# Feed-forward's last group: where the running sum of squares is added

## The reference

```python
def rmsnorm(x, g):
    y = x * rsqrt(mean(x * x, axis=-1) + EPS)
    return y * g

def swiglu(x, w_gate, w_up, w_down):
    return (silu(x @ w_gate) * (x @ w_up)) @ w_down

# layer
x = x + 0.5 * swiglu(rmsnorm(x, n_f1), f1_g, f1_u, f1_d)
h = rmsnorm(x, n_mix)
...                       # two mixers of h, merged
x = x + merged @ w_o
x = x + 0.5 * swiglu(rmsnorm(x, n_f2), f2_g, f2_u, f2_d)
# end
y = rmsnorm(x, norm_final)
```

## Time and profile before

| what | value |
|---|---|
| median of 3 timed runs | 3586.05 us (3582.97 to 3590.58) |
| the profiled execution | 3583.59 us |
| its span, from the first to the last instruction | 3581.8 us |
| TensorE busy | 3382.4 us, 94% of the span |
| VectorE busy | 1156.0 us, 32% |
| ScalarE busy | 1000.0 us, 28% |
| GpSimd busy | 935.5 us, 26% |
| mean granted TensorE clock | 0.959 |

### The profile page before, as it was taken

The page is one execution under the profiler, slowest core; times in us unless marked ns, Lnnn a source line. Parts: engine busy times, 40 slices in busy tenths (PEclk is TensorE's granted clock), DMA queues, the critical chain, the costliest instruction groups (busy, mean ns, idle before and its releaser), DMA issues. The chain is left out here.

```text
span 3581.8 us, 52005 instructions
## 1 busy us (share of the span) xinstructions
PE 3382.4 (94%) x20610; PEld 3291.5 (92%) x20610; DVE 1156.0 (32%) x1780; ACT 1000.0 (28%) x1461; POOL 935.5 (26%) x520
## 2 busy tenths in 40 slices
PE   6999999996999799999999999769997999999997
PEld 6999999996999699999999999649997999999996
DVE  4232223224566333232232222142323232223223
ACT  5111111114333344444354342220123111111112
POOL 3112121214222323333233331211235112221212
PEclk8999999998999899999999999559998999999998
DMA  3111111102222212121121220245412111111101
GB/s 122 47 35 53 41 41 41 47 18 88 81 84 91 66 50 71 50 69 52 57 77 45 62 64 23 68 138 184 142 42 59 48 41 47 41 47 41 38 26 50
DMA packets 274431, 222.74 MB, mean 62 GB/s; under 512 B 12043, under 2 KB 251787, under 8 KB 274289
## 3 DMA queue, kind: packets, MB, share of 16 engines
q1 hardware_dynamic: 273988, 220.56, 20.4%
q10 hardware_dynamic: 324, 0.41, 0.0%
HBM read 170.66 MB, written 50.28 MB: 62 GB/s over the span
## 5 line engine op out<-in xcount | busy, mean ns | idle before, releaser
L163 PE MATMUL ffn_bank<-ffn_h_hi,ffn_w_hi 128*128 128x368 f32 x2112 | 699.1, 331 | 41.7 <-DVE ffn_h_lo L428 33.2
L164 PE MATMUL ffn_bank<-ffn_h_lo,ffn_w_hi 128*128 128x368 f32 x2112 | 700.3, 332 | 0.0
L165 PE MATMUL ffn_bank<-ffn_h_hi,ffn_w_lo 128*128 128x368 f32 x2112 | 699.0, 331 | 0.0
L163 PE MATMUL mix_bank<-mix_h_hi,mix_w_hi 128*128 128x368 f32 x1752 | 629.7, 359 | 24.0 <-DVE mix_h_lo L1028 18.3
L385 POOL TENSOR_TENSOR ffn_w_lo<-ffn_w_raw,ffn_w_hi 128x1024 fp32r<-128x1024 f32 x132 | 315.0, 2394 | 1174.4 <-ACT ffn_w_hi L381 1174.2
L165 PE MATMUL mix_bank<-mix_h_hi,mix_w_lo 128*128 128x368 f32 x1752 | 579.1, 331 | 0.0
L164 PE MATMUL mix_bank<-mix_h_lo,mix_w_hi 128*128 128x368 f32 x1752 | 579.0, 330 | 0.0
L163 PEld LDWEIGHTS ffn_bank<-ffn_h_hi,ffn_w_hi 128*128 128x128 f32 x2112 | 399.2, 189 | 42.9 <-issue 42.9
L746 POOL TENSOR_TENSOR mix_w_lo<-mix_w_raw,mix_w_hi 128x1024 fp32r<-128x1024 f32 x73 | 200.2, 2742 | 780.9 <-ACT mix_w_hi L741 780.9
L165 PEld LDWEIGHTS ffn_bank<-ffn_h_hi,ffn_w_lo 128*128 128x128 f32 x2112 | 398.8, 189 | 0.0
L164 PEld LDWEIGHTS ffn_bank<-ffn_h_lo,ffn_w_hi 128*128 128x128 f32 x2112 | 398.3, 189 | 0.0
(11 more groups left out here) (292 smaller groups left out, 4512.6 us busy)
## 6 DMA issues: line engine op xcount, KB each, us to landing
mix_w_raw<-in_w_in SPq DMA_DIRECT2D x73, 512.0 KB, 6.2
ffn_w_raw<-in_ffn_w_gate SPq DMA_DIRECT2D x44, 512.0 KB, 3.8
ffn_w_raw<-in_ffn_w_up SPq DMA_DIRECT2D x44, 512.0 KB, 3.8
ffn_w_raw<-in_ffn_w_down SPq DMA_DIRECT2D x44, 512.0 KB, 3.5
scratch_qkv<-mix_out SPq DMA_DIRECT2D x24, 552.0 KB, 2.8
scratch_x<-g_x SPq DMA_DIRECT2D x8, 552.0 KB, 7.8
scratch_z<-turn_z_out SPq DMA_DIRECT2D x8, 552.0 KB, 2.8
scratch_sig_a<-turn_gate_out SPq DMA_DIRECT2D x8, 552.0 KB, 2.7
```

What stands on the lines that cost most here:

```text
L163: pe.matmul(out, w_hi, x_hi, start=first, stop=False)
L164: pe.matmul(out, w_hi, x_lo, start=False, stop=False)
L165: return pe.matmul(out, w_lo, x_hi, start=False, stop=last)
```

## The change

The 24 additions to the running sum leave GpSimd's queue and go into VectorE's, each one step late: behind the x addition n, the wait for it and the return of its bank, VectorE adds square n - 1. The 24th sum addition stands behind the loop. The helper `add_part` with its two waits is the same, and so are the squares, the ones matmuls and the factors. `ffn` is called twice, so both blocks change.

```diff
@@ -464,9 +464,6 @@
                 w.split_lo(pool, 0, GROUPS - 1, u)
             pool.wait_ge(h_ready[0], KC // 2)
             nrm.clear(pool)
-            for b in range(NB):
-                for c in range(KC):
-                    nrm.add_part(pool, b, c)
 
         @block.tensor
         def _(pe):
@@ -609,6 +606,9 @@
                 add(0, GROUPS - 1, c, b, n).then_inc(x_final, 1)
                 dve.wait_ge(x_final, n + 1)
                 dve.sem_inc(bank_free[n % 6], 1)
+                if n:
+                    nrm.add_part(dve, (n - 1) // KC, (n - 1) % KC)
+            nrm.add_part(dve, NB - 1, KC - 1)
```

## The result

| | before | changed |
|---|---|---|
| median, 20 runs each | 3587.93 us (3582.97 to 3592.36) | 3592.03 us (3586.34 to 3594.87) |
| ratio | 1 | 1.0013, 95% interval 1.0007 to 1.0019 |
| the profiled execution, and its span | 3583.59, 3581.8 us | 3586.34, 3584.6 us |
| VectorE busy | 1156.0 us | 1176.7 us |
| GpSimd busy | 935.5 us | 887.6 us |

The change makes the kernel slower by 0.13%, some 4.7 us (2.5 to 6.8 by the interval; the medians are 4.1 apart): smaller than what the prediction called a difference, but clear of none over 20 runs. The forecast was +0.9 us, 3587.0 in a range of 3581 to 3592; the measured 3592.03 lies just outside.

The account below looks back on a forecast made before the run. VectorE was to take over from GpSimd as the pace of each block's last group, at 0.68 + 0.46 = 1.14 us a step. Squares 0.46 and 0.43 us later, +0.9 on 3586.05, gave 3587.0 us, range 3581 to 3592.

Parts of the forecast that it names:

- the 24th square: ScalarE's last square in each feed-forward block: what follows hangs on it; forecast 0.46 and 0.43 us later than before.
- The step: VectorE's time per part in the last group: 0.68 us plus 0.46 us, 1.14 us in all.
- Both are over: I cost them at nothing: The sum addition's two new waits, for square n-1 and sum n-2, were taken as already met and costing nothing.
- one satisfied wait more or less is not seen here: Feed-forward and merge-stage pairs with different waits both showed 0.68 us, so 0.68 was taken from x to sum addition.
- the 0.9 of the sum: Forecast delay of the whole kernel from both feed-forward blocks together: +0.9 us.
- the upper bound, 0.06 for two waits: Most that two further waits before the sum addition were allowed to add to the 0.68 us: 0.06 us.
- The cover: TensorE in the last group: six banks of 1.0 us each keep it from stalling, though the 24th x addition comes 2.5 us late.
- TensorE paces: Rival: sum additions fit into VectorE's waits for TensorE in the last group; -4.2 us, 3581.8 us; chance 0.12.
- the wait on itself is free: Rival: VectorE's wait for its own x addition costs nothing, step 1.08 us; -2.0 us, 3584.0 us; chance 0.10.
- The longer step: Rival: each sum addition delays the next x addition 0.68 us, step 1.36; +10.6 us, 3596.6 us; chance 0.08.
- its point of decision: VectorE's step of 1.29 us, past which the kernel would be slower by more than 0.2% (7.2 us).
- The rule that the prediction weighed: A VectorE operation starts only once the one before left the pipe, and semaphores cost nothing extra; the prediction rejected both halves.

Follow-up runs that it names:

- e2: Changed kernel with sum addition n-1 in front of the wait for x addition n and its bank's return; ratio to the kernel before 0.9985, again 0.9983.
- e1: Changed kernel with each sum addition's two waits moved in front of the wait for the x addition; ratio to the kernel before 1.0021.
- e4: Changed kernel with the additions reading the square twice and writing a spare tile, the sum preset to a constant; one run, 3588.61 us.
- e5: Changed kernel with the sum addition's two waits early, closed off by an increment of an unused semaphore; ratio to the kernel before 1.0004.
- e3: Changed kernel with two more long-satisfied waits in front of each of the first 23 sum additions; ratio to the kernel before 1.0020.
- e6: Changed kernel with the bank's credit behind the sum addition instead of in front of it; ratio to the kernel before 0.9987.

## Why the prediction was off

**What paces, before and after: right.** GpSimd was the slowest of the four before, VectorE is after. That the 24th square sets the end of the block stands shown: over all kernels of the table it moved between 23.8 and 30.7 us after the first x addition, and the next stage followed 10.43 to 10.47 us behind it. Two blocks in twenty are the exception, both of kernel e2, with 10.30 and 10.16 us: there the first matmul by ones behind the squares took 0.79 and 0.68 us in place of 0.95.

**The step, term by term.** From the sum addition to the next x addition: 0.46 forecast, 0.46 measured. From the x addition to the sum addition: 0.68 forecast, 0.76 measured, and this is the term that failed. "Both are over: I cost them at nothing" took a wait whose condition holds for a wait without a cost. And "one satisfied wait more or less is not seen here" was read out of two pairs that are alike in the one thing that counts. Both have one queue instruction between them: the credit in the feed-forward pair, and in the merge pair of the earlier trace rows a register operation, which has a row of its own in the trace of before:

```profile
L2012 DVEq FUSED_REGOPS  x24: 57/57/75, 2535.2 to 2615.9; - x24
```

The change puts a second one there. The 0.08 us come 22 times until the 24th square in each block, 1.8 us, 3.5 in all; with the 0.9 of the sum that is 4.4. Even the upper bound, 0.06 for two waits, was below it.

**A pause of 0.36 us** makes up the rest of the 4.7. It occurs once, in the second block, in front of one sum addition, where the idle time is 0.58 us in place of 0.23:

```profile
3540.70 0.53 DVE L597 SCALAR_TENSOR_TENSOR g_x<-ffn_bank,g_x 128x368 f32<-128x368 f32 x1
3541.82 0.54 DVE L336 TENSOR_TENSOR g_rstd<-g_rstd,ffn_hid 128x368 f32<-128x368 f32 x1 [0.58 <-ACT ffn_hid L330]
```

The square named there can't be the cause, since the one that this addition reads was over by 3540.56. The changed kernel run again, e1, e4 and e5 have the pause at the same step of the second block; e3 has one in each block, of 0.42 and 0.38 us, at other steps; before, e2 and e6 show none. What it is stays open.

**The level.** The forecast stood on the median of three runs, 3586.05; over 20 runs the same kernel has 3587.93. Of the 5 us between 3587.0 and 3592.03, 1.9 are this, 3.5 the queue instruction and 0.4 the pause; the sum is larger than the difference by less than the medians are certain. The level alone, or the queue instruction and the pause alone, would have left the time inside the range; it took both to pass its upper end. The profiled execution alone would have misled: its two blocks are 4.7 us longer, but it is only 2.75 us longer as a whole, because the stages in between differ by a few us from one execution to the next. From the last square of the first block to the first x addition of the second it is 2670.1 us before, 2668.2 in the changed kernel, and up to 2675.3 (e6) over the ten traces, more than what the change moves.

**The cover: right.** No contention appeared: the additions have 541 to 545 ns. The granted clock in the 8 us from 3543 on is 0.62, 0.64 before. TensorE did not stall in the changed kernel; its last down matmul starts 22.86 us after the first x addition, 22.85 before. In e3, where VectorE falls further behind, they do come late: its last parts start 1.32 us apart (845.73, 847.05, 848.37), VectorE's step, and the end follows VectorE all the same.

**The rivals.** That TensorE paces was given 0.12 and did not happen: in that order of the queue VectorE was the slower. e2 shows that the time was there: by its squares 4.3 us, 4.2 worked out. That the wait on itself is free did not come: the wait stands with 0.23 us in front of the sum additions. The longer step (1.29 or more) did not come either: 1.22 lies between the forecast and its point of decision, inside the 1.24 that the range allowed.

The rule that the prediction weighed was not given whole there, so its rows do not speak against it as it says. The Trainium skill ("VectorE: DVE Perf Modes", section "The DRAIN you can't avoid") adds in the same paragraph: "A next op that is not held starts earlier". The trace of e2 agrees with that: its operations follow each other after 0.45 to 0.46 us though each has 0.53 to 0.54. That a semaphore costs nothing extra, the Trainium skill measured, in the same section, with one after each operation. In e2, too, every operation counts up a semaphore, and the next still comes 0.45 to 0.46 us later. What costs here is a wait for the operation in front: 0.11 us (0.57 against 0.46) if the next operation carries it, as in e6, and 0.1 more for each queue instruction in between.

## What to carry to other kernels

In these runs a wait that is long over was free only while the engine worked. Behind a wait of an engine on its own last operation each instruction of its queue counts, some 0.1 us each on VectorE here, so put independent work, not waits and credits, directly behind the operation. When an operation is moved onto an engine that then paces, write down that engine's queue instruction by instruction, and try both sides of its waits: in this kernel the same 24 additions cost 4.7 us or gave back 4.3, counted by the squares, by the order of a few lines.

## What the runs showed of the hardware

- On VectorE an operation of 0.53 to 0.54 us lets the next start 0.45 to 0.46 us after its own start if nothing waits for its end (e2), and 0.57 if the next carries that wait itself (e6).
- A queue instruction that is recorded with 21 to 50 ns adds 0.08 to 0.11 us where nothing covers it (0.57, 0.68, 0.76, 0.86 us in e6, e5, the changed kernel and e3), and nothing where an operation runs beside it (e2, e6).
- Several waits can ride on one queue instruction (50 ns in place of 21, e3), so that moving lines can pack them anew: e1 moved two waits forward and got slower.
